# Two-block transformer kernel: gates and branches token-major, decay columns in one slab, the last modulation part's rows moved

## What is computed

```python
# modulation vectors: 3 parts of 2048 in block 1, 6 parts in block 2
mod = silu(c) @ w_ada + b_ada                      # [2048] @ [2048, 3*2048]
h = rmsnorm(x, pre_g) * (1 + scale) + shift
q, k, v, gate_a, u, gate_p = split(h @ w_in)
y_a = windowed_gqa(q, k, v, rel_table, sink) * silu(gate_a)      # [256, 1024]
y_p = multiscale_pool(u, w_pool_grp, pool_scale) * silu(gate_p)  # [256, 1024]
g_a, g_p = split(sigmoid(h @ w_merge + b_merge))                 # two of [256, 2048]
merged = g_a * (y_a @ w_br_attn) + g_p * (y_p @ w_br_pool)
x = x + gate * rmsnorm(merged @ w_out, post_g)
# block 2: mod = silu(c_2) @ w_mod + b_mod, then the token mixer
q_a, k_a, v_a, q_b, k_b, v_b, gk_lr, og_b, g_a, g_b = split(h @ w_in_2)
o_a = sliding_window_attention(rope(q_a), rope(k_a), v_a)
gk  = log_sigmoid(gk_lr @ w_gk_up + b_gk) / 16     # gk_lr: the 16 "decay columns"
o_b = rmsnorm(gla_chunked(q_b, k_b, v_b, gk)) * silu(og_b)
merged = sigmoid(g_a) * (o_a @ w_br_a) + sigmoid(g_b) * (o_b @ w_br_b)
x = x + g1 * rmsnorm(merged @ w_out_2)
# block 2: feed-forward, hidden width 5632
u = causal_conv3(h @ w_up); gate, val = split(u)
x = x + g2 * rmsnorm((silu(gate) * val) @ w_down)
```

## Time and profile before

| | us |
|---|---|
| median of three runs | 2401.97 |
| lowest and highest | 2399.42, 2407.26 |
| the profiled execution's own time | 2391.19 |
| its span in the profile | 2389.4 |
| PE busy (share of the span) | 2258.8 (95%) |
| DVE busy | 1731.5 (72%) |
| ACT busy | 1103.2 (46%) |
| granted TensorE clock, mean | 0.965 |

### The profile page before, as it was taken

The page is one execution under the profiler, slowest core; times in us unless marked ns, Lnnn a source line. Parts: engine busy times, 40 slices in busy tenths (PEclk is TensorE's granted clock), DMA queues, the critical chain, the costliest instruction groups (busy, mean ns, idle before and its releaser), DMA issues.

```text
span 2389.4 us, 29806 instructions
## 1 busy us (share of the span) xinstructions
PE 2258.8 (95%) x12112; PEld 1926.1 (81%) x12112; DVE 1731.5 (72%) x2035; ACT 1103.2 (46%) x1423; POOL 76.9 (3%) x101
## 2 busy tenths in 40 slices
PE   5499999999999899999999989999999999999998
PEld 3488888888877778888888878877888888888886
DVE  6958867777876677766777788887777777784443
ACT  3243356664444554443455543455444444443332
POOL 0000000000000000000011110000000000000000
PEclk8599999999998999999999999998999999999999
DMA  9877878877984756668877779885655555556553
GB/s 382 323 265 273 299 247 282 293 276 260 293 299 161 265 180 225 229 207 309 284 251 237 245 262 321 323 293 204 184 183 188 188 182 193 179 193 246 194 194 124
DMA packets 244398, 581.55 MB, mean 243 GB/s; under 512 B 11931, under 2 KB 14799, under 8 KB 238885
## 3 DMA queue, kind: packets, MB, share of 16 engines
q1 hardware_dynamic: 232608, 535.93, 65.1%
q0 software_dynamic: 10464, 41.27, 5.0%
q10 hardware_dynamic: 1188, 2.44, 0.3%
HBM read 560.70 MB, written 18.90 MB: 243 GB/s over the span
## 4 chain that ended last, share of the span: by engine, by line
PE 71%; DVE 14%; DMA 10%; ACT 3%; issue 2%; ACTq 0%; DVEq 0%
PE gemm L1778 35%; PE gemm L1779 18%; DMA mod_stage<-in_w_mod 5%; DVE w_lo L1087 5%; PE gemm L1743 3%; PE gemm L1741 3%; PE gemm L1742 3%; DVE mod_acc L1081 3%; PE gemm L1782 2%; DMA w_stage<-in_w_ada 2%; PE extra L1568 1%; PE gemm L1781 1%; ACT w_hi L739 1%; DMA mod_stage<-in_w_ada 1%; DVE mod_acc_scale L1065 1%
## 5 line engine op out<-in xcount | busy, mean ns | idle before, releaser
L1778 PE MATMUL gemm<-operand_main,w_hi 128*128 128x512 f32 x4087 | 1475.3, 402 | 35.3 <-DVE proj L1456 19.5
L1087 DVE TENSOR_TENSOR w_lo<-w_stage,w_hi 128x1024 fp32r<-128x1024 f32 x736 | 860.9, 1211 | 421.9 <-ACT w_hi L739 421.5
L1779 PE MATMUL gemm<-operand_main,w_lo 128*128 128x256 f32 x4087 | 1152.6, 282 | 0.0
L739 ACT ACTIVATE w_hi<-w_stage 128x1024 fp32r<-128x1024 f32 x736 | 731.7, 1044 | 768.4 <-PE gemm L1779 554.2
L1778 PEld LDWEIGHTS gemm<-operand_main,w_hi 128*128 128x128 f32 x4087 | 776.2, 190 | 217.9 <-DVE w_lo L1087 31.4
L1779 PEld LDWEIGHTS gemm<-operand_main,w_lo 128*128 128x128 f32 x4087 | 779.9, 191 | 12.1
L1081 DVE SCALAR_TENSOR_TENSOR mod_acc<-mod_stage,c_silu,mod_acc 128x1024 f32<-128x1024 f32 x210 | 267.5, 1300 | 62.4 <-DMA mod_stage<-in_w_mod 48.2
L1741 PE MATMUL gemm<-w_hi,ffn_hidden 128*128 128x512 f32 x352 | 136.9, 389 | 0.0
L1742 PE MATMUL gemm<-w_lo,ffn_hidden 128*128 128x512 f32 x352 | 136.9, 389 | 0.0
L1743 PE MATMUL gemm<-w_hi,ffn_hidden 128*128 128x512 f32 x352 | 136.9, 389 | 0.0
L1782 PE MATMUL gemm<-operand_main,w_hi 128*128 128x512 f32 x281 | 111.9, 398 | 0.0
(11 more groups left out here) (235 smaller groups left out, 1922.7 us busy)
## 6 DMA issues: line engine op xcount, KB each, us to landing
w_stage<-in_w_in SPq DMA_DIRECT2D x128, 1024.0 KB, 6.4
mod_stage<-in_w_mod SPq DMA_DIRECT2D x192, 512.0 KB, 6.0
w_stage<-in_w_up SPq DMA_DIRECT2D x88, 1024.0 KB, 5.1
w_stage<-in_w_down SPq DMA_DIRECT2D x44, 1024.0 KB, 5.0
w_stage<-in_w_merge SPq DMA_DIRECT2D x32, 1024.0 KB, 5.4
w_stage<-in_w_out SPq DMA_DIRECT2D x32, 1024.0 KB, 8.8
w_stage<-in_w_ada SPq DMA_DIRECT2D x31, 1024.0 KB, 7.6
mod_stage<-in_w_ada SPq DMA_DIRECT2D x32, 512.0 KB, 6.0
```

The costliest lines, as they stand in the source:

```text
L739: return nc.scalar.activation(o, i_, f, **kw)
L1087: tt(WL[:, slot_of(n), c0:c1], WST[:, slot_of(n), c0:c1], WH[:, n % HIS, c0:c1].bitcast(F32), ALU.subtract)\
L1778: mm(G[:, m, :], hi, x_of(k), start=(k == 0), stop=False)
L1779: ins = mm(G[:, m, T:2 * T], lo, x_of(k)[:, 0:T], start=False, stop=False)
```

## The change

1. `merge`, `branch1`, `gates2`, `branch2` and the v columns of the last two `qkvb` phases go to the row form: 32 + 16 + 32 + 24 + 16 = 120 slabs. Neighbouring row groups take the banks 0, 1 and 2, 3 in turn. Gates of block 1: DVE adds a bias row, loaded by POOL as 256 KB a phase, and ACT makes the sigmoid as before. Gates of block 2: ACT makes the sigmoid straight from PSUM, DVE has no part. v of the GLA heads: ACT copies it straight out, and the 32 transposes and 8 copies of the heads are gone. Branches: DVE multiplies PSUM by the gate (2 instructions), and for the second operand multiplies and adds (4), in place of 4 and 6; ACT has none. Gates stand in DRAM in lines of 4 KB.
2. The merged result now stands tokens by features, so PE transposes it (`merged_turn`, 32 transposes a block), ACT and DVE split it from the `extra` banks (`merged_split`); half of it in the last branch phase, half in the first output phase.
3. `gk` is one slab of 16 chunks by 128 columns.
4. Modulation rows: part 4 now 2 rows a phase in `branch1` and 3, 3, 2, 0 in `out1`; part 8 gets an accumulator of its own (`mod_acc_last`) and 2 rows in each of `up` 0 to 7, its `mod_end` behind `up` 7; `branch2` 3 and `out2` have none. `out_gate` 2 and its store move from `up` 1 to `up` 8.

```diff
     def __init__(self, w, col, slabs, operand, evac, tiles=QUAD, chunks=QUAD, **kw):
+        self.chunks = chunks
+        self.size = chunks * self.cols
...
-            phases.append(Phase("merge", i, [Group(w_merge, 512 * i, 4, "main", "gate", bias=col["b_merge"] + 4 * i, slot=4 * i)],
+            phases.append(Phase("merge", i, [Group(w_merge, 512 * i, 4, "main", "gate_row", blk=0, slot=i)],
...
-                                hooks=behind, mod=(4, i, 1)))
+                                hooks=behind, mod=(4, 2 * i, 2), slots=(0, 2)))
...
-                                mod=(4, 4 + 3 * i, 3),
-                                pre=[] if i else [("prep_merged", 0)], post=[("resid", 0)] if i == 3 else []))
+                                hooks=behind, mod=(4, 8 + 3 * i, (3, 3, 2, 0)[i]), post=[("resid", 0)] if i == 3 else []))
...
-        phases.append(Phase("gk", 0, [Group(w_in2, 5632, 4, "main", "proj", tiles=1, tile=59)]))
+        phases.append(Phase("gk", 0, [Group(w_in2, 5632, 1, "main", "proj", tiles=1, chunks=KT, tile=59)]))
...
+            if i >= 2:
+                qkvb = [Group(w_in2, 1536 + 1024 * i + 512 * n, 4, "main", "v_row", h=2 * i - 4 + n) for n in range(2)]
...
-                                mod=((7, 6, 3), (7, 9, 3), (7, 12, 4), (8, 0, 4))[i], slots=(4, 2, 3, 0) if i else (2, 3, 4),
+                                mod=((7, 6, 3), (7, 9, 3), (7, 12, 4), None)[i], slots=(4, 2, 3, 0) if i else (2, 3, 4),
...
-                                pre=[] if i else [("prep_merged", 1)], mod=(8, 4 + 3 * i, 3), post=[("resid", 1)] if i == 3 else []))
+                                hooks=behind, post=[("resid", 1)] if i == 3 else []))
...
-                                hooks=behind, pre=[] if b else [("prep_h", 2)]))
+                                hooks=behind, pre=[] if b else [("prep_h", 2)], mod=(8, 2 * b, 2) if b < 8 else None, slots=(1, 6),
+                                post=[("mod_end", 8)] if b == 7 else []))
...
+                g.in_rows = g.evac in ROWS_OUT
+                g.side = 1 - before.side if g.in_rows and before.in_rows else 0
+                g.by_act = g.evac == "v_row" or g.evac == "gate_row" and g.kw["blk"] == 1
...
+                if g.by_act:
+                    for h in range(2):
+                        wait_full(act, g, h)
+                        if g.evac == "v_row":
+                            ins = activate(VT[g.kw["h"]][:, h, :], row_bank(g, h), ACT.Copy)
+                        else:
+                            positive(act, gate_stored, 16 * gate_no[g.gi])
+                            ins = activate(GST[1][:, h, :], row_bank(g, h), ACT.Sigmoid)
+                        ins.then_inc(act_done, 1)
...
+                if g.evac in ("merge_a", "merge_b"):
...
+                    for h in range(2):
+                        wait_full(dve, g, h)
+                        o = MERGED[:, h, columns_of(n % 4)] if b else MA[:, h, :]
+                        tt(o, row_bank(g, h), GL[:, b, h, :], ALU.mult).then_inc(pair_done, 1)
+                        if b:
+                            wait_evac(dve, g, h + 1)
+                            tt(o, o, MA[:, h, :], ALU.add).then_inc(merge_tiles, 1)
...
+                if name == "merged_turn":
+                    blk, j = arg
+                    pe.wait_ge(merge_tiles, 8 * blk + 2 * j + 2)
+                    for p in (2 * j, 2 * j + 1):
...
+                                ins = nc.tensor.transpose(X[p % 4][:, at0:at0 + P], MERGED[:, h, t * P:(t + 1) * P], IDENT[:, :])
+                        ins.then_inc(merged_turned, 1)
...
+                if g.operand == "merged" and ph.i == 0:
+                    pe.wait_ge(op_ready, op_count[name] - 8 + 2 * q + 2)
```

269 lines of the change are left out of this document (137 added, 132 removed).

## The result

| | us |
|---|---|
| median after, four runs (lowest, highest) | 2328.0 (2325.86, 2331.77) |
| median before, beside it, four runs | 2400.69 (2393.93, 2407.26) |
| ratio, 95% interval | 0.9699 [0.9669, 0.9729] |
| the profiled execution after, its span | 2325.86, 2324.1 |
| the profiled execution before, its span | 2391.19, 2389.4 |

The change makes the kernel 3.0% faster. The predicted 2339 (2317 to 2368) is 11 us too high, with the right sign and the time inside the range. The sum itself, 63.3 us less for the profiled execution, stands against 65.3 measured.

What follows compares the result with a forecast made beforehand. PE's own work was taken as the bound (busy 95%, 71% of the chain), the rest mostly waits for DVE. Terms summed to 63.3 us less: 2391.2 to 2327.9 profiled, plus 10.8 gives 2339 us, range 2317 to 2368.

Steps and rivals of the forecast that it cites:

- (a): In the 120 slabs changed to row form: pace goes from 5.654 to 5.440 us a slab, 25.7 us less.
- (b): On PE: 64 transposes come for the merged result, 32 of the v heads go, 3.6 us more.
- (c): At `gk` and `q2`: one slab of decay columns ends most of PE's 6.79 us idle time, 7.8 us less.
- (d): After `out1` and `out2`: without modulation rows in the last phase, the residual stages start earlier, 14.0 us less together.
- (e): Behind `up` 7: `mod_end` 8 moves to where nothing hides it, 4.3 us more.
- (f): In `out1`: waits for the bank and rows go, 5 us of DVE waits in the first phase stay, 7.0 us less.
- (g: In `out2`: without its 12 modulation rows DVE's work falls to half, 0.5 us of waits stays, 7.3 us less.
- h: In `branch2`: fewer evacuation instructions and no rows in the last phase; of 13.6 us of waits 6 stay, 7.6 less.
- i): In `gates2`: gate evacuation moves from DVE to ACT; of 9.3 us of waits 4 stay, 5.3 less.
- (j): In `up`: two modulation rows a phase cost 0 in `up` 1 to 7 (DVE 88% busy), 2.5 us more in `up` 0.
- (k): In `branch1`: one modulation row more a phase, DVE then busy 19 of 21.8 us, 1.0 us more.

## Why the prediction was right

**The pace (a)** holds. ACT's copies in `merge`, released by PE, 5.44 apart:

```profile
445.86 2.01 ACT L779 ACTIVATE w_hi<-w_stage 128x1024 fp32r<-128x1024 f32 x2 [3.07 <-PE gemm L1779]
451.30 2.01 ACT L779 ACTIVATE w_hi<-w_stage 128x1024 fp32r<-128x1024 f32 x2 [3.43 <-PE gemm L1779]
```

`merge` fell by 6.9 for 32 slabs, and its DMAs (300 GB/s, share 0.86) had the room that the step says. It was right to take a measured pace over one worked out from columns; why the forms differ was not known then, and half of the difference still is not. The Trainium skill, page "TensorE: Matmul & The Clock Gate", section "Back-to-back issue gap", gives N / 2.4 + 2.5 ns for the gap of a single matmul, and says itself that it does not hold for a stream of weight loads and matmuls, which is what runs here. So the prediction's estimate from it (5.18 and 5.20 us a slab) asked more of the page than it states. By the halved matmuls a matmul costs 13.3 ns beside its columns here, not 2.5, and the page's 131 ns for 512 columns in such a stream is not met either (5.44 us / 24 = 227 ns).

**The transposes (b)** are the right size, in other places than a single sum tells: eight cost 0.9 of PE's pace (slabs of 6.33 to 6.36 against 5.44), 7.2 for 64, and the v heads' 32 (4.1 us, all in `gates2` before) have gone.

**The decay columns (c)**: the 6.79 us of PE idle time in the earlier trace rows are 1.02 now, the evacuation that the step named as next:

```profile
761.22 0.39 PE L1820 MATMUL gemm<-operand_main,w_hi 128*128 128x512 f32 x1
762.63 0.47 PE L1816 MATMUL gemm<-operand_main,w_hi 128*128 128x512 f32 x1 [1.02 <-DVE proj L1501]
```

**The residual stages (d)**: -7.4 and -5.9 against a joint -11.5. After `out1` PE's last matmul starts at 717.93, the sum of part 4 follows it at once (3.63 us against 6.99 in the earlier trace rows), and the second `gained_rows` starts 1.2 us after that matmul's start, where it was 10.0:

```profile
718.16 3.63 PE L1597 MATMUL extra<-ones,mod_acc 128*128 128x1 f32 x32
...
731.55 0.39 PE L1816 MATMUL gemm<-operand_main,w_hi 128*128 128x512 f32 x1
...
719.13 0.69 DVE L1460 TENSOR_TENSOR gained_rows<-gemm,gain_row 128x512 f32<-128x512 f32 x1 [1.35 <-ACT square_work L779]
```

`kv2` starts 13.6 us after the last `out1` matmul, where it was 21.0. The kernels with rows in `out1` 3 have `kv2` at 42.5 to 45.0, those without at 36.0 to 37.6.

**`mod_end` 8 (e)** was priced at 4.3 and cost 6.4 at `up` 8. The windows of the last slab of `up` 7, of `mod_end`, and of what follows:

```profile
1926.85:1932.50 5.65, 5.65 (x35) 4.90 (x34) 4.59 (x8) 2.61 (x3) 0.00 (x0) 1.00 0.58 188
1932.50:1936.30 3.80, 3.80 (x33) 3.80 (x32) 3.58 (x9) 2.49 (x3) 0.00 (x0) 0.86 0.66 216
1936.30:1942.10 5.80, 5.80 (x19) 4.93 (x20) 4.23 (x6) 0.00 (x0) 0.00 (x0) 0.50 0.10 40
1942.10:1947.70 5.60, 5.60 (x34) 4.91 (x33) 1.73 (x2) 2.82 (x3) 0.00 (x0) 1.00 0.29 84
```

The sum itself takes 4.15 us (1932.34). Before it ends the clock falls, and it is 0.50, 1.2 GHz, for 5.8 us in which the slab's own matmuls run. That is the missing 2. The step took the sum's own duration and left out the matmuls behind it. It does not happen behind every such sum: behind `mod_end` 5 the same kernel keeps 1.00 (see `og` below).

**`out1` (f)** is the one step that failed; the time stayed in the range because others made up for it. "What stays is DVE in the first phase [...] I leave 5": 98.9 - 16 x 5.44 - 1.8 for the transposes is 10.1, and 9.4 of it is `out1` 0, which is 33.0 and without its rows 23.6. The 26 us of work that the step counted were not the cause (with the rope work moved out of it, 0.8 less). The step counted DVE's instructions and not the transfers they wait for: 3.9 us of waiting for one row, and PE waited 5.8 us for the split behind it and ran at a mean clock of 0.90. Step a had worked out that a `branch1` phase with two rows needs 337 GB/s, found that it "just fits", and did not ask what the store and the 3 MB of gain and residual rows at the same seam do to a phase with little room. How the wait for the row divides between these and the single pair of `mod_stage` halves stays open. The rest of f came: 6.5 less in the other three phases.

**`out2`, `branch2`, `gates2` (g, h, i)**: -5.9, -13.3, -13.4 against -5.5, -10.9, -15.7. One wait of PE for a gate group's evacuation was 4.9 in the earlier trace rows; after, PE's group of matmuls in `gates2` with all such waits (count, busy, mean ns, idle before) has 1.5:

```profile
L1777 PE MATMUL gemm<-w_hi,operand_main 128*128 128x512 f32 x256 | 102.0, 398 | 1.5 <-DVE gate_out L1504 1.5
```

`og`, for which nothing was predicted, lost 4.0. Of this 3.2 is one slab, the one behind `mod_end` 5: 12.36 us before, 9.12 after, with the granted clock at 0.88 over `og` 1 before (1077.0 to 1106.4) and 1.00 after (1049.3 to 1075.2). The variants made from the kernel after have 96.3 to 99.4 for `og`, so this is mostly the luck of one execution and no gain of the change.

**Rows in `up` (j)**: `up` 1 to 7 at 45.2 each with DVE busy 275.0 of 316.6 us, 87%, as walked through; the 2.5 for `up` 0 were probably too much (with rows 60.9 in the run that moved part 8 alone, 62.0 after, 67.9 before), but no run separates them from the residual stage. **`branch1` (k)** lost nothing by its second row, and `branch1` 0 was 2.6 shorter, 0.9 of it pace; the other 1.7 no term had, and their cause is open.

**From the profile to the median.** 10.8 us were added for the distance of the profiled execution of before to its median. After, the distance is 2.1, and the kernel before, run beside the experiments, had medians of 2392.9 to 2395.3, 2 to 4 above that profile. The first three runs happened to lie high. With 3 for 10.8 the same sum gives 2331, so most of the 11 us by which the forecast is high is this term and none of the kernel.

**What was luck.** Line by line the table misses by 13.0 us one way (`og` 4.0, `branch1` 2.5, `branch2` 2.4, and smaller ones) and by 11.0 the other (`out1` 5.1, `gates2` 2.3, `qkvb` 1.8, and smaller ones). That the sum comes within 2 us is the cancelling of these. The signs and sizes of the large terms, pace, decay columns, residual stages and `out2`, are not luck; runs with one part alone show them. The prediction's own range is also added up wrongly: its parts, -7 or +13, +-3, and -0 or +3, give 2329 to 2358 and not 2323 to 2356. The wider range that it forecasts, 2317 to 2368, does not hang on this.

## What to carry to other kernels

Before work is moved into a phase, add up its bytes as well as its instructions: a phase at 346 GB/s and a share of 0.96 has little room (the DMAs reached 394 to 403 here). A third row in two phases still fitted, one more did not. A wait taken away at such a place can come back at the next one, as 11.9 us for 9.4 in one version, so judge by the sum over all stretches that share the transfers. In an in-order queue the place of an instruction counts more than the busy share: the same rows in `up` cost nothing at slabs 1 and 6 and 21.5 us at slabs 3 and 7.

## What the runs showed of the hardware

- A store of 8 KB in single fp32 values (three of them in the kernel after) took 12.6, 14.3 and 16.1 us to land. Behind the first (14.3) the DMAs moved 70 GB/s at a share of 0.75 for 12 us, and 394 right after. With the store a phase earlier the low rate came with it, 91 GB/s for 10 us.
- After 32 matmuls of one column (4.15 us, `mod_end` 8) the matmuls behind them ran at a granted clock of 0.50 for 5.8 us, though PE is busy in all of that time. `up` 8 took 50.0 to 51.9 us in all runs with this sum in front of it, and 45.2 without. Behind `mod_end` 5 the clock fell in the kernel before (0.88 over 29.4 us) and not in the kernel after (1.00).
- Two matmuls of 256 columns, each with its weight load, in place of one of 512 cost 13.3 ns more; 32 matmuls of 512 and 256 columns in the feature-major form took 0.107 us a slab more than that price explains.
